# Sample queries spread as three bf16 parts by one product, and a softmax step moved two attention units later

## The reference

```
q_b, k_b, v_b, z_u, z_v, q_c, gates = split(rmsnorm(x) @ w_in)       # q_b: 12 heads x 64, q_c: 4 heads x 128
logits_b = q_b . cached window keys / 8 + bias      # per request: 3 head groups x 128 keys, plus the token's own key
logits_c = q_c . cached memory keys / sqrt(128)     # per request: 256 keys, 4 heads
p = softmax(logits);  out = p . cached values
x = x + (sig(gA)*A(z_u, z_v) + sig(gB)*B + sig(gC)*C) @ w_out        # then a 32-expert feed-forward layer, top 4
```

## Time and profile before

| | us |
|---|---|
| Median of 3 runs (lowest, highest) | 1539.71 (1538.79, 1542.64) |
| The profiled execution | 1539.54 |
| its span, first to last instruction | 1537.7 |
| mean granted TensorE clock | 0.953 |

### The profile page before, as it was taken

One profiled execution on the slowest core, in us unless ns is written; L12 is line 12 of the kernel. 1 busy time (PEld: TensorE's weight loads), 2 busy tenths in 40 slices (PEclk: granted clock), 3 DMA queues, 4 the chain that ended last, 5 costly groups with the idle time before them and its releaser, 6 DMA issues.

```text
span 1537.7 us, 20357 instructions
## 1 busy us (share of the span) xinstructions
PE 1409.7 (92%) x8013; PEld 693.9 (45%) x8013; DVE 374.8 (24%) x858; ACT 240.7 (16%) x389; POOL 52.6 (3%) x90
## 2 busy tenths in 40 slices
PE   3999977997898779999999999999999999999995
PEld 1685535866786334343343433333343333333333
DVE  2100365420012152222222212222221222222123
ACT  2001011220001041121111111111121111112112
POOL 0100212002100000000000000000000000000000
PEclk9999877996599989999999999999999999999998
DMA  9535966239247657999999999999999999999994
GB/s 319 181 128 191 328 236 237 89 157 345 94 163 288 261 207 310 424 422 421 422 422 422 421 423 421 422 422 422 422 422 422 422 422 422 421 422 422 422 422 164
DMA packets 86697, 515.17 MB, mean 335 GB/s; under 512 B 10047, under 2 KB 11655, under 8 KB 36812
## 3 DMA queue, kind: packets, MB, share of 16 engines
q1 hardware_dynamic: 77504, 493.69, 79.3%
q0 software_dynamic: 6016, 18.83, 3.8%
q10 hardware_dynamic: 3148, 2.24, 0.5%
HBM read 511.21 MB, written 47.52 MB: 363 GB/s over the span
## 4 chain that ended last, share of the span: by engine, by line
PE 65%; DMA 21%; DVE 5%; SPq 4%; issue 2%; ACT 1%; ACTq 1%; POOL 0%; DVEq 0%
PE psum L524 62%; DMA weights<-in_w_gate_up 17%; SPq L424 4%; PE psum L527 3%; DMA weights<-in_w_out 2%; DMA weights<-in_cache_mem_kv 2%; DVE qk L1272 1%; ACTq L1325 1%; ACT qk L1328 0%; POOL weights L484 0%; DVE x L1297 0%; DVE kvt L1166 0%; DVE va L1179 0%; DVE hT L1242 0%; DVE kc L1177 0%
## 5 line engine op out<-in xcount | busy, mean ns | idle before, releaser
L524 PE MATMUL psum<-weights,wsp 128*64 128x512 f32 x2048 | 491.8, 603 | 15.2 <-DMA weights<-in_w_gate_up 14.4
L524 PE MATMUL psum<-weights,merged 128*64 128x512 f32 (+2 forms) x1152 | 274.3, 600 | 10.7 <-DMA weights<-in_w_out 9.2
L524 PEld LDWEIGHTS psum<-weights,wsp 128*64 128x64 f32 x2048 | 127.5, 136 | 266.8 <-issue 177.9
L1242 DVE TENSOR_TENSOR hT<-psum,hT 128x264 f32<-128x264 f32 x264 | 101.7, 427 | 529.4 <-PE psum L524 529.3
L524 PE MATMUL psum<-hT,weights 128*128 128x264 f32 x704 | 171.7, 403 | 13.8 <-DVE weights L984 9.1
L524 PEld LDWEIGHTS psum<-weights,merged 128*64 128x64 f32 (+2 forms) x1152 | 89.6, 141 | 167.0 <-issue 158.9
L524 PEld LDWEIGHTS psum<-hT,weights 128*128 128x128 f32 x704 | 138.2, 198 | 45.6 <-DVE weights L984 12.2
L524 PE MATMUL psum<-bT,merged 64*128 64x264 f32 x528 | 94.2, 434 | 1.1 <-ACT merged L1487 0.7
L1468 ACT COPY bT<-psum 128x264 f32<-128x264 f32 x33 | 12.5, 379 | 484.1 <-PE psum L527 484.0
L524 PEld LDWEIGHTS psum<-bT,merged 64*128 64x128 f32 x528 | 39.8, 184 | 106.7 <-issue 103.9
L1272 DVE TENSOR_SCALAR qk<-psum,lowest 128x512 f32<-128x512 f32 x64 | 48.0, 750 | 162.6 <-PE psum L524 159.2
(11 more groups left out here) (242 smaller groups left out, 765.3 us busy)
## 6 DMA issues: line engine op xcount, KB each, us to landing
weights<-in_w_gate_up SPq DMA_DIRECT2D x256, 1024.0 KB, 26.1
weights<-in_w_down SPq DMA_DIRECT2D x128, 1024.0 KB, 25.0
out<-in_cache_win_kv SPq DMA_DIRECT2D x8, 4094.0 KB
weights<-in_w_in SPq DMA_DIRECT2D x13, 2048.0 KB, 7.7
weights<-in_cache_mem_kv POOLq DMA_DIRECT2D x16, 512.0 KB, 7.8
out<-in_cache_win_kv SPq DMA_DIRECT2D x2, 4088.0 KB
weights<-in_cache_win_kv POOLq DMA_DIRECT2D x48, 128.0 KB, 6.1
weights<-in_w_mem_kv SPq DMA_DIRECT2D x2, 2048.0 KB, 14.4
```

Source lines behind the costliest of these rows:

```text
L524: return nc.tensor.matmul(out, lhsT, rhs, start=start, stop=stop, **kw)
L1242: V.tensor_tensor(acc[:, c, :], p_a[j % 2][part], acc[:, c, :], ALU.add).then_inc(s_acc, 1)
```

## The change

`pick_b` is a bf16 table of 96 x 8 with ones at rows b, 32+b and 64+b of column b. `q_parts` is a bf16 tile of 96 x 1280, zeroed by GpSimd, that holds the queries as three bf16 parts: the rounded value in rows 0 to 7, the rounded rest in rows 32 to 39, what then is left in rows 64 to 71. One bf16 product with column b of `pick_b` adds the three parts and spreads them. ScalarE makes the casts, VectorE the two subtractions (`qrest`, `qlow`). `zv` 0 moves ahead of them; so each other large job moves one request earlier against `norm_v`, which stays before request 3. The window part of a request becomes one step `sk` of 768 columns in `wide[0]` or `wide[1]`, outside the rotating banks, with one multiplication and one sum on VectorE. The second half of `slog`, from the wait for the maximum on, becomes a step `stop` at n = 2 of the attention units; `ssum` moves from n = 4 to n = 5.

```diff
-    s += [("qs", 0), ("qs", 1), ("qcs",), ("vts",), ("selfb",)]
     big = [("zv", t) for t in range(3)] + [("zu", m) for m in range(4)]
+    s += [("qs", 0), ("qs", 1), ("qcs",), big[0], ("qrest",), ("vts",), ("qlow",), ("selfb",)]
+    big = big[1:]
     for b in range(NS):
         if b == 3:
             s += [("norm_v",)]
-        s += [("sk", b, 0), ("sk", b, 1), ("skc", b)]
+        s += [("sk", b), ("skc", b)]
...
-        if n == 4:
+        if n == 2:
+            s += [("stop",)]
+        if n == 5:
             s += [("ssum",)]
...
+        q_parts = scratch[0:PARTS * E, 3584:4224].bitcast(BF16)
+        q_mid = scratch[0:NS, 4224:4864].bitcast(BF16)
+        q_rest = scratch[0:NS, 4864:6144]
...
+            nc.gpsimd.memset(q_parts, 0.0).then_inc(s_qzero, 1)
...
                 elif kind == "sk":
-                    b, n = a
-                    taken(pe, "qcs")
-                    last = mm(o[:, 0:384], ident[0:NS, b:b + 1].to_broadcast([NS, P]), qs[:, n * 384:(n + 1) * 384])
+                    b, = a
+                    if b == 0:
+                        pe.wait_ge(s_qmid, 2)
+                        pe.wait_ge(s_qlow, 1)
+                    if b >= 2:
+                        pe.wait_ge(s_qread, b - 1)
+                    spread = pick_b[:, b:b + 1].to_broadcast([PARTS * E, P])
+                    mm(wide[b % 2][:, 0:512], spread, q_parts[:, 0:512])
+                    mm(wide[b % 2][:, 512:BW], spread, q_parts[:, 512:BW]).then_inc(s_qspread, 1)
                 elif kind == "skc":
-                    last = mm(o, ident[0:NS, a[0]:a[0] + 1].to_broadcast([NS, P]), qs[:, BW:BW + 512])
+                    last = mm(o, pick_b[:, a[0]:a[0] + 1].to_broadcast([PARTS * E, P]), q_parts[:, BW:BW + 512])
...
+                    V.tensor_copy(pick_b[:], quarters[0:PARTS * E, 0:NS])
...
+                elif kind == "qrest":
+                    dve.wait_ge(s_qhi, 1)
+                    V.tensor_tensor(q_rest, qs, q_parts[0:NS, :], ALU.subtract).then_inc(s_qrest, 1)
+                elif kind == "qlow":
+                    dve.wait_ge(s_qmid, 1)
+                    V.tensor_tensor(q_parts[2 * E:2 * E + NS, :], q_rest, q_mid, ALU.subtract).then_inc(s_qlow, 1)
...
                 elif kind == "sk":
-                    b, n2 = a
-                    if n2 == 0:
-                        dve.wait_ge(s_kvin[b % 2], 64 * (b // 2 + 1))
-                    ready()
-                    kk = kv_b[b % 2].rearrange("p g c -> p (g c)")[:, n2 * 384:(n2 + 1) * 384]
-                    V.tensor_tensor(prod[:, 0:384], kk, o[:, 0:384], ALU.mult).then_inc(free, 1)
-                    own()
-                    seq(V.tensor_reduce(sB[:, b * NH + 6 * n2:b * NH + 6 * n2 + 6], prod[:, 0:384].rearrange("p (h c) -> p h c", c=HD),
-                                        AX.X, ALU.add))
+                    b, = a
+                    dve.wait_ge(s_kvin[b % 2], 64 * (b // 2 + 1))
+                    dve.wait_ge(s_qspread, b + 1)
+                    V.tensor_tensor(prod[:, 0:BW], kv_b[b % 2].rearrange("p g c -> p (g c)"), wide[b % 2][:, 0:BW], ALU.mult).then_inc(s_qread, 1)
+                    dve.wait_ge(s_qread, b + 1)
+                    seq(V.tensor_reduce(sB[:, b * NH:(b + 1) * NH], prod[:, 0:BW].rearrange("p (h c) -> p h c", c=HD), AX.X, ALU.add))
...
                     dve.sem_inc(s_done["lgs"], 1)
+                elif kind == "stop":
                     dve.wait_ge(s_done["parmax"], 1)
...
+                elif kind == "qcs":
+                    for x in (("qs", 0), ("qs", 1), ("qcs",)):
+                        taken(act, *x)
+                    act.wait_ge(s_qzero, 1)
+                    A.copy(q_parts[0:NS, :], qs).then_inc(s_qhi, 1)
+                elif kind == "qrest":
+                    act.wait_ge(s_qrest, 1)
+                    A.copy(q_mid, q_rest).then_inc(s_qmid, 1)
+                    A.copy(q_parts[E:E + NS, :], q_rest).then_inc(s_qmid, 1)
...
-                elif kind == "slog":
+                elif kind == "stop":
                     act.wait_ge(s_done["lgs"], 2)
```

More of the change, by code:

```diff
@@ L155 @@
 ROTATING = {"vec", "wsp", "rel", "sbias", "memT", "kc", "xT", "vc", "kct", "q", "k", "v", "kt", "qc", "qs", "qcs", "vts",
-            "selfb", "sk", "skc", "zv", "zu", "vat", "sp", "p", "g", "ssum", "sv", "wos", "wo", "woz", "xt", "rt", "lg", "pos"}
+            "selfb", "skc", "zv", "zu", "vat", "sp", "p", "g", "ssum", "sv", "wos", "wo", "woz", "xt", "rt", "lg", "pos"}
 LAST_USE = {("kc", 3): 0, ("vc", 1): 1, ("q", 3): 2, ("k", 1): 3, ("k", 5): 4, ("v", 2, 0): 5, ("v", 2, 1): 6, ("qc", 3): 7,
@@ L237, in build @@
         ones = sb("ones", [P, P])
+        pick_b = sb("pick_b", [PARTS * E, NS], BF16)
         wspT = sb("wspT", [P, AG, P])
@@ L336, in build @@
         s_kvin = [sem(f"kv_in{n}") for n in range(2)]
+        s_qzero, s_qhi, s_qrest, s_qmid, s_qlow, s_qspread, s_qread = (
+            sem("sample_q_" + n) for n in ("zeroed", "high", "rest", "mid", "low", "spread", "read"))
         s_kvout, s_kvcout, s_vaout = sem("out_kv"), sem("out_memkv"), sem("out_chunk_v")
```

## The result

| | before | after |
|---|---|---|
| Median of 5 runs (lowest, highest), us | 1539.71 (1538.56, 1542.64) | 1531.73 (1527.61, 1532.98) |
| The profiled execution | 1539.54 | 1527.61 |
| its span | 1537.7 | 1525.6 |
| mean granted clock | 0.953 | 0.955 |

The ratio is 0.9938, 95% interval 0.9919 to 0.9957: faster by 8.0 us, where 18.4 had been forecast (1521.2 us, range 1513 to 1530). Two repetitions, on chips 1 and 15, gave 0.9897 (0.9878 to 0.9915) and 0.9911 (0.9890 to 0.9932), or 14.6 and 12.8 us by the medians. Why the first comparison shows less is open: its median of before is the lowest of all batches, its median of after the highest. The profiled execution was the fastest of its five; its span is 12.1 us shorter.

The account below looks back on a forecast made before the run. TensorE's work was taken to bound the kernel before its last third, which weight transfers bind. Gains of 9.1 us (spread and order) and 9.3 (moved softmax half) summed to 18.4, from 1539.6 to 1521.2 us, range 1513 to 1530.

Parts of the forecast that it names:

- The moved softmax half: Second half of slog two units later: 8.07 us wait gone, 2.07 from the clock, less 0.8 for ssum, 9.3 gained.
- a sign of being wrong: At stop in the attention units: GpSimd's maximum coming later than VectorE; forecast over in 6.4 us, some 3 us to spare.
- `ssum`: Attention units: moved before a p job, its cover shrinks by 1.8 us; a loss of 0.8 taken between 0 and 1.8.
- The spread: Ahead of slog: bf16 spreads and new order bring slog 16.2 us earlier without waits, 10.2 with late streams, 9.1 after clock loss.
- The failed step: Before request 7: stream 7's last part issued at 223.4 takes 7.6 us, landing at 231.0 where VectorE is ready at 228.8.
- the 1.1 us taken off for `zv` 1: Ahead of slog: half of the 2.25 us zv 1 costs if the pause before it lowers the clock.
- rival 2: Before request 7: stream 7 falls behind the copy, landing at 245.5, slog at 255.5; net gain 5.0 us, 1534.6; chance 0.08.
- rival 1: Ahead of slog: no stream is late, 16.2 + 9.3 = 25.5 us gained, 1514; chance 0.17.
- The rule of turns: DMA engines alternate queues by packet, so a stream would not stand behind the whole copy; stream 7 as near 18.7 as 7.6.
- One to one at the end: What the stretch before 261 us gains or loses moves later weight and copy issues and comes out fully at the end.
- rival 3: At stop: GpSimd's maximum takes longer than 10 us and VectorE stands before it, giving back 9.3 us; 1530; chance 0.07.
- rival 4: TensorE stays at 1.2 GHz through 172 to 222 and into the units: 12 us slower, 1552; chance 0.06.

Follow-up runs that it names:

- hold_pad_ssum: After, with block 13 and both copies held until all keys are read, the vts turns made three times, and ssum back at n = 4: 1520.80 us, ratio 0.9856.
- stop_only: Before, with only the softmax step moved (stop at n = 2, ssum at n = 5): 1532.15 us, ratio 0.9940.
- order_only: Before, float32 spreads and whole softmax, with zv 0 ahead of the turns and each other large job one request earlier: 1540.50 us, ratio 0.9989.
- again: After, unaltered, run a second time beside before: 1527.46 us, ratio 0.9897.
- again2: After, unaltered, run once more beside before on another chip: 1530.41 us, ratio 0.9911.
- pad: After, with the twelve turns of the samples' values (vts) made three times, 24 small TensorE products more: 1530.13 us, ratio 0.9917.
- copies_later: After, with the two window-cache copies behind blocks 12 and 13 issued behind block 14 instead: 1541.45 us, ratio 0.9986.
- spread_only: After, with stop directly behind slog and ssum at n = 4 again, so only the spread and its order: 1540.23 us, ratio 0.9994.
- before_hold: Before, with block 13 and its copy held until all requests' keys are read and block 12's copy moved behind it: 1542.84 us, ratio 1.0004.
- hold_spread: After with softmax whole behind slog and ssum at n = 4, plus block 13 and both copies held until all keys are read: 1532.23 us, ratio 0.9931.

## Why the prediction was right and wrong

**The moved softmax half: right.** The stall of 8.07 us went (none is left before the product, 0.29 before its weight load) and the next g job takes 3.72 us instead of 5.90. GpSimd's maximum came later than I had it: it was over at 255.6, 10.6 us behind the first half of slog instead of 6.4, and VectorE waited 1.53 us where I saw 3 us to spare. I had named this as a sign of being wrong; it cost TensorE 0.28 us. `ssum` was mis-sized: I took 0.8 us between 0 and 1.8; TensorE's new stall behind it is 2.07 us where before had one of 0.22, and hold_pad_ssum, with 0.22 again, shows that it need not be paid. In sum 9.3 forecast; block 14 (wc) is issued 14.75 us earlier (276.06 for 290.81) where slog's first half was 6.1 earlier, so 8.7, and 9.9 alone in stop_only.

**The spread: its working right, its streams wrong.** `zv` 0 at 163.9 (164.3), request 0 at 175.4 (175.5), request 2 at 191.8 (191.2), norm_v at 196.4 (195.9): the walk holds to within 0.8 us up to there. The failed step is "the last part of stream 7 is issued at 223.4, while the block is still under way and the copy not yet: 7.6 us, 231.0". The pair was issued at 224.4 and that part at 225.5; it took 9.7 us and landed at 235.2:

```profile
196.93 18.73 DMA weights<-in_cache_mem_kv
...
225.50 9.67 DMA weights<-in_cache_mem_kv
```

Of the 4.2 us that it landed late, 2.1 are the later issue, since stream 4 came at 215.7, not 213, and 2.1 the longer flight. The 7.6 us were the flight of a part issued 0.4 us behind the block, and I gave them to one that my own walk put 3.1 behind. The profiles have what lies between. With block and copy, a last part took 7.6 to 8.0 us when issued 0.4 us behind the block (before, stop_only, order_only), 8.6 to 9.7 at 1.0 to 1.1 us (again, again2, after), 16.0 at 2.7 (pad) and 16.9 to 19.6 at 5.6 to 8.0. With the block but no copy it took 10.3 at 1.5 us (copies_later) and 6.1 to 7.1 at 5.7 (copies_later and three runs with the hold). So stream 4 was late by the copy, and stream 7 in after mostly by the block. By the row of pad, the 3.1 us of my walk would have cost some 16 us: that it came no worse is luck, since `zu` 3 ended at 224.4 and not at 220.3.

So slog's first half ended at 245.1 (forecast 241.0, or 242.1 with the 1.1 us taken off for `zv` 1), 6.1 us earlier than before instead of 9.1. I had set the point from which rival 2 decides at 6 us behind the block, from the earlier trace rows; pad showed 2.7 us to be enough. With the margin this thin, an execution can fall on either side, which fits the scatter of spread_only over 11 us; but only the profiled executions show their streams, and that this moves the medians is argued.

With the race taken out (before_hold, hold_spread) the spread's half is worth 10.6 us and both 21.3: between my forecast and rival 1's 25.5. Rival 1 had 16.2 for that half. Counted from the turns of the memory queries, slog's first half ends 14.5 us earlier in hold_spread than in before_hold, block 14 is issued 12.8 us earlier, the last expert's second product comes 12.5 us earlier and the end 10.4. So 1.7 us of the 16.2 were not there, 1.7 went up to block 14, most of it behind a maximum that VectorE awaits for 9.22 us instead of 8.00, and 2.1 in the last turns. The mechanism of the spread was right; the stream's term was mis-sized because the block's and the copy's part in its flight was taken too small.

**The rule of turns.** I wrote that the Trainium skill, "DMA: Bandwidth & Descriptors", section on queues, rings and completion order, lets each engine take turns between its queues packet by packet, and concluded that a stream would then not stand behind the copy. The trace agrees with the rule, as far as the profile's packets are the page's (17 packets against 18, and 198 against 197), and not with my conclusion: at 65,504 bytes a packet a turn each is 1.11 MB for 0.07.

**Later stages.** "One to one at the end" failed by a little. Block wb is issued 13.4 us earlier, wc was 14.75: 1.1 of that are the waits for the samples' values (9.90 + 12.95 + 4.81 us against 9.50 + 12.71 + 4.39). At the end the pauses in the last turns, a term that the sum doesn't have, cost 2.4 us (31.7 against 29.3); the experts had given back 1.1 before that. From 13.4 at the experts' start to 12.1 at the end.

**The other rivals.** The maximum took the 10 us of rival 3 but held VectorE for no more than 1.5 us, and the clock was granted in full from 251 to 261 and at 0.96 from 163 to 204 (rival 4, against 0.83 before). The jobs behind a pause were slow, as in the earlier trace rows (`zv` 1 8.17 us, `zu` 2 6.58, `zu` 3 5.39), and the branch-A jobs behind slog were not (g 3.72 us each).

**The sum.** 18.4 forecast, 12.1 in the profiled spans: 3.0 us are the streams, 0.6 the softmax half, 1.3 the values, 1.3 the end. The timed median is 4.1 us above the profiled execution, because that one was the fastest of five; what made the other four longer no trace shows.

## What to carry to other kernels

When a change makes a consumer faster, walk the transfers that feed it as carefully as the engines, and give every place where a small transfer meets a large copy within a few microseconds a chance of falling behind it. Take a transfer's flight from a row with the same lag behind its neighbours, not from the nearest one at hand: here 0.4 and 2.7 us of lag made 7.6 and 16.0 us. Holding the copy until the last small transfer had been used recovered the whole loss (8.0 us), with the copy still over before the next stage that reads; moving it further only moved the price.

## What the runs showed of the hardware that was not expected

Two DMA queues with work waiting shared the engines packet against packet in the stretches shown (17 to 18; 198 to 197), at both packet sizes, so that packets of 65,504 bytes beside packets of 3 to 4 KB took 94% of the bytes; cut to 2,944 bytes they took 47%.

A pause of TensorE that the profile puts down to "issue" moved with the number of instructions ahead of it, without any change in the work around it (between the ninth and tenth of 24 turns, and away with 48 instructions more). It ended 1.3 to 1.5 us after a packet of 16,384 bytes on an "instruction" queue had landed, in all ten profiles that have it. That the number of instructions decides it rests on one amount of padding. The Trainium skill, "Runtime: NRT & Kernel Launch", section on instruction fetch mechanics, says that an engine's instructions are refilled block by block and that a taken branch to a block not at hand has to wait for it. The 24 turns stand right behind a conditional branch of TensorE, and a block boundary within them would give such a second pause, by my own inference: the page calls the crossing of a boundary mostly hidden. The trace fits the wait, with the packets above and 0.8 to 1.6 us for the second pause, but doesn't name it.

In copies_later SyncE stood 20.28 us in the issue of one copy behind block 15, with the three copies issued at 278 us ahead of it; the same instruction took 0.59 us in after. What it waited for there was not tried.
